# Strassen's algorithm for the gate and up products of two 512-feature blocks in each SwiGLU of a two-layer encoder trunk, with the feed-forward loops written out

## The reference, cut to what matters

```python
def _swiglu(h, w_gate, w_up, w_down):
    return (jax.nn.silu(h @ w_gate) * (h @ w_up)) @ w_down
...
        x = x + 0.5 * _swiglu(_rms_norm(x, ffn1_norm[l]), ffn1_w_gate[l], ffn1_w_up[l], ffn1_w_down[l])
```

## Time and profile before

| | us |
|---|---|
| median of 3 runs | 1047.45 (1047.15 to 1047.8) |
| span of the profiled execution, first to last instruction | 1045.7 |
| TensorE busy | 1040.6 |
| VectorE busy | 687.1 |
| ScalarE busy | 593.7 |
| DMA, mean | 200 GB/s, 208.81 MB |

### The profile page before, as it was taken

How to read it: one execution, slowest core, us unless ns; L and a number is a source line. 1 busy time by engine, 2 the same in 40 slices (tenths; PEclk the granted TensorE clock), 3 DMA queues, 4 the chain that set the end, 5 groups by cost and what they waited for, 6 DMA issues and landing times.

```text
span 1045.7 us, 13767 instructions
## 1 busy us (share of the span) xinstructions
PE 1040.6 (100%) x5001; PEld 872.2 (83%) x5001; DVE 687.1 (66%) x911; ACT 593.7 (57%) x792; POOL 248.9 (24%) x258
## 2 busy tenths in 40 slices
PE   9999999999999999999999999999999999999998
PEld 6888888998888888888888888889988888888887
DVE  6755655698976766555576555656999677656551
ACT  6754544576874665445466454536778557645440
POOL 2960000148850000000048300002588300000000
PEclk9999999999999999999999999999999999999999
DMA  8977666455644696675569667565366366976641
GB/s 280 310 237 234 186 211 200 143 200 172 210 163 125 206 313 188 206 232 196 153 191 282 216 206 228 184 199 172 122 212 224 118 191 222 261 221 186 207 139 41
DMA packets 191555, 208.81 MB, mean 200 GB/s; under 512 B 64112, under 2 KB 162704, under 8 KB 191504
## 3 DMA queue, kind: packets, MB, share of 16 engines
q1 hardware_dynamic: 190288, 206.03, 63.6%
q10 hardware_dynamic: 1216, 2.11, 0.7%
HBM read 192.90 MB, written 1.05 MB: 185 GB/s over the span
## 4 chain that ended last, share of the span: by engine, by line
PE 98%; ACT 1%; DVE 1%; issue 0%; POOL 0%; ACTq 0%
PE bank L663 31%; PE bank L665 31%; PE bank L664 31%; PE bank L744 1%; PE bank L905 1%; PE bank L914 1%; PE bank L935 1%; PE bank L670 1%; PE bank L702 0%; PE bank L913 0%; PE bank L937 0%; DVE htok L1563 0%; DVE x L1611 0%; ACT htok L1132 0%; PE bank L923 0%; PE bank L963 0%
## 5 line engine op out<-in xcount | busy, mean ns | idle before, releaser
L1517 DVE TENSOR_TENSOR wlo<-raw,whi 128x2048 fp32r<-128x2048 f32 (+2 forms) x152 | 347.4, 2290 | 82.6 <-ACT whi L1123 81.5
L663 PE MATMUL bank<-whi,hThi 128*128 128x512 f32 (+1 forms) x976 | 378.4, 388 | 0.0
L665 PE MATMUL bank<-whi,hTlo 128*128 128x512 f32 (+1 forms) x976 | 373.7, 383 | 0.0
L664 PE MATMUL bank<-wlo,hThi 128*128 128x512 f32 (+1 forms) x976 | 373.6, 383 | 0.0
L1123 ACT ACTIVATE whi<-raw 128x2048 fp32r<-128x2048 f32 (+2 forms) x176 | 335.3, 1910 | 16.8 <-DMA raw<-in_ffn_w_up 7.3
L665 PEld LDWEIGHTS bank<-whi,hTlo 128*128 128x128 f32 x976 | 183.3, 188 | 35.7
L663 PEld LDWEIGHTS bank<-whi,hThi 128*128 128x128 f32 x976 | 183.4, 188 | 35.1 <-issue 0.3
L664 PEld LDWEIGHTS bank<-wlo,hThi 128*128 128x128 f32 x976 | 183.4, 188 | 34.8
L1216 ACT ACTIVATE gates<-bank,small 128x256 f32<-128x256 f32 x88 | 41.8, 475 | 263.5 <-PE bank L665 262.8
L663 PE MATMUL bank<-whi,gThi 128*128 128x512 f32 (+1 forms) x416 | 162.2, 390 | 0.0
L664 PE MATMUL bank<-wlo,gThi 128*128 128x512 f32 (+1 forms) x416 | 161.1, 387 | 0.0
(11 more groups left out here) (177 smaller groups left out, 823.6 us busy)
## 6 DMA issues: line engine op xcount, KB each, us to landing
raw<-in_ffn_w_down SPq DMA_DIRECT2D x88, 512.0 KB, 4.2
raw<-in_ffn_w_gate SPq DMA_DIRECT2D x84, 512.0 KB, 4.3
raw<-in_ffn_w_up SPq DMA_DIRECT2D x84, 512.0 KB, 5.4
raw<-in_w_in SPq DMA_DIRECT2D x48, 512.0 KB, 4.8
raw<-in_w_out SPq DMA_DIRECT2D x16, 512.0 KB, 4.4
raw<-in_w_in SPq DMA_DIRECT2D x8, 544.0 KB, 4.5
raw<-in_w_mla_out SPq DMA_DIRECT2D x8, 512.0 KB, 3.9
raw<-in_w_conv_out SPq DMA_DIRECT2D x8, 512.0 KB, 4.7
```

Of the source, the lines that this page charges most:

```text
L663: nc.tensor.matmul(out, lh, rh, start=start, stop=False, skip_group_check=skip)
L664: nc.tensor.matmul(out, lh, rl, start=False, stop=False, skip_group_check=skip)
L665: return nc.tensor.matmul(out, ll, rh, start=False, stop=stop, skip_group_check=skip)
L1517: nc.vector.tensor_tensor(wlo[:, slot(u0, RING), 0:n], raw[:, slot(u0, RAW), 0:n], whi[:, slot(u0, RING), 0:n].bitcast(F32), ALU.subtract) ...
```

## The change

In each feed-forward, chunks 3 and 4 together, and 6 and 7 together, become one block of 512 features. With A the input (two row tiles by two channel halves) and B the weights (gate and up, 512 columns each, by two channel halves), four quarters each, the block's [gate up] is A times B by Strassen's algorithm in Winograd's form: 7 products of a 128 x 512 quarter with a 512 x 512 quarter instead of 8, each 4 k-steps x 3 matmuls. Three of them take a weight quarter as it is (B11, B22, B21), four take sums of quarters (T1 to T4).

- **Weights.** The upper quarters of gate and up go to two buffers of their own (chain[0], chain[1], over htok and ktok) and not to the raw slots. VectorE forms T1, T3, T2 and T4 in place (`add_T1` and so on, 128x2048 each); ScalarE rounds and VectorE takes the remainder of each of the 7 as a unit.
- **Inputs.** Once in each feed-forward VectorE adds hThi and hTlo (`whole_rows`, 128x2048), makes four mixed quarters (`mixed_rows`, 4 of 128x512), ScalarE rounds them (`mixed_round`, 128x2048) and VectorE takes the remainder (`mixed_rest`, 128x2048).
- **Outputs.** Within a block ScalarE copies four banks out (`keep`, 128x512), VectorE does four sums of 128x512 (`up_first`, `gate_first`, `up_second`, `gate_second`), two silus and two gated products of 128x512 replace four of each of 128x256. Both row tiles of both chunks are complete only after T4.
- **Orders.** All loops are written out, with a new order of calls on each engine. gain, bias, vtok and cu share one region with the mixed input quarters; cu's margin is cleared once a layer. Units, raw slots and counters are renumbered for this.

Within the lists below, `gate_split`, `down_split` and `lower` are the same ScalarE or VectorE steps as `split` before, for a unit of gate and up, of w_down, and for B22 and B21; `first_of` and `sum_of` are ScalarE's rounding of chain buffers, `of_chain` VectorE's remainder of them. The hunks stand in the order SP, TensorE, ScalarE, VectorE, after the constants.

```diff
--- before.py
+++ after.py
+BLK = (3, 6)
+CW = 2 * FC
+PRODUCTS = ("B11", "T1", "D0", "T2", "B22", "B21", "T3", "T4", "D1")
...
+        chain = (htok[:, 0:2048], heads[:, 0:2048])
...
+        mixed = flat[:, 512:2560].rearrange("p (k n) -> p k n", k=KD)
+        kept = [flat[:, 512 + i * CW:512 + (i + 1) * CW] for i in range(4)]
...
+                b = per_block(l, f, c) - 1
+                if b % len(BLK) == 0:
+                    if i == 0:
+                        sp.wait_ge(sq_ready, per_norm(l, 2 * f, 1))
+                    elif l or f:
+                        sp.wait_ge(block_joined[1], nth_norm(l, 2 * f, 0) + 1)
+                else:
+                    last = unit_block(f, BLK[b % len(BLK) - 1], "T3" if i else "T4")
+                    sp.wait_ge(wlo_ready, l * U_LAYER + last + 1)
+                dst = chain[i].rearrange("p (k n) -> p k n", k=4)
+                src = quarter_of((wg, wu)[i][f], l, c, 0)
+                for k in (0, 2):
+                    sp.dma_start(dst[:, k:k + 2, :], src[:, k:k + 2, :]).then_inc(chain_landed[i], 16)
...
+                gate_up(l, f, 2, 0)
+                gate_up(l, f, 2, 1)
+                down(l, f, 0)
+                chain_load(l, f, 3, 0)
+                down(l, f, 1)
+                chain_load(l, f, 3, 1)
+                lower_load(l, f, 3, "B22")
+                turn(0)
+                lower_load(l, f, 3, "B21")
+                turn(1)
+                turn(2)
+                down(l, f, 2)
+                gate_up(l, f, 5, 0)
+                gate_up(l, f, 5, 1)
+                chain_load(l, f, 6, 1)
+                chain_load(l, f, 6, 0)
+                down(l, f, 3)
+                down(l, f, 4)
+                lower_load(l, f, 6, "B22")
+                turn(3)
...
+                def block_product(c, name, b, lhs, start=True, stop=True):
+                    u = unit_block(f, c, name)
+                    unit_waits(pe, l, u)
+                    for k in range(4):
+                        ins = products(bank[:, b, :], lhs(k), wt(u, 2048, 4, k, slice(0, CW)),
+                                       start=start and k == 0, stop=stop and k == 3, skip=True)
+                    ins.then_inc(unit_free, 1)
+                def mixed_T(h, t):
+                    def of(k):
+                        cols = slice(t * P, (t + 1) * P)
+                        return sThi[:, 4 * h + k, cols], sTlo[:, 4 * h + k, cols]
+                    return of
+                def strassen(c):
+                    done = per_block(l, f, c)
+                    again = c != BLK[0]
+                    def plain_T(h, t):
+                        return lambda k: hT(4 * h + k, t)
+                    if again:
+                        pe.wait_ge(kept_ready, (done - 1) * 4)
+                    else:
+                        pe.wait_ge(gu_ready, per_gu(l, f, 2, 0))
+                    block_product(c, "B11", 4, plain_T(0, 0))
+                    if again:
+                        pe.wait_ge(c12_ready, done - 1)
+                    else:
+                        pe.wait_ge(gu_ready, per_gu(l, f, 2, 1))
+                        pe.wait_ge(mixed_ready, l * 2 + f + 1)
+                    block_product(c, "T1", 5, mixed_T(1, 1))
+                    down(c - 2, 0)
+                    down(c - 2, 1)
+                    pe.wait_ge(kept_ready, (done - 1) * 4 + 1)
+                    block_product(c, "T2", 4, mixed_T(0, 0), start=False)
+                    pe.wait_ge(kept_ready, (done - 1) * 4 + 2)
+                    block_product(c, "B22", 5, mixed_T(1, 0), start=False)
+                    pe.wait_ge(gu_ready, per_gu(l, f, 5 if again else 1, 0))
+                    block_product(c, "B21", 6, plain_T(1, 0))
+                    pe.wait_ge(kept_ready, (done - 1) * 4 + 3)
+                    block_product(c, "T3", 4, mixed_T(0, 1), start=False)
+                    pe.wait_ge(gu_ready, per_gu(l, f, 5 if again else 1, 1))
+                    block_product(c, "T4", 7, plain_T(1, 1))
+                    down(c - 1, 0)
+                    down(c - 1, 1)
...
                 first()
-                pair(2, 2)
-                pair(3, 3)
-                with pe.Fori(0, (NCH - 5) // 2) as i:
-                    pair(i * 2 + 4, 4)
-                    pair(i * 2 + 5, 5)
+                pair(2)
+                strassen(3)
+                pair(5)
+                strassen(6)
+                pair(8)
+                pair(9)
                 last()
...
+                def mixed_round():
+                    act.wait_ge(mix_step, (l * 2 + f + 1) * 5)
+                    nc.scalar.activation(sThi[:, :, :], mixed, ACT.Copy).then_inc(mixed_hi, 1)
...
+                def block_first(c):
+                    sum_of(c, "T2")
+                    lower(c, "B22")
+                    lower(c, "B21")
+                    keep(c, 0, "B11")
+                    sum_of(c, "T3")
+                    keep(c, 1, "T1")
+                    sum_of(c, "T4")
+                    round_joined(c - 1)
+                    down_split(c - 1)
+                    keep(c, 2, "T2")
+                    gate_split(c + 2, 0)
+                    gate_split(c + 2, 1)
...
+                def block_second(c):
+                    block_silu(c, 0)
+                    keep(c, 3, "T3")
                     split_planes(c, 0)
-                    silu(c, 1)
-                    split(l, u + 2, i)
+                    down_split(c)
+                    block_silu(c, 1)
                     split_planes(c, 1)
                 first()
...
-                    pair(i * 2 + 2, 2, i * 2)
-                    pair(i * 2 + 3, 3, i * 2)
+                down_split(0)
+                silu(1, 0)
+                first_of(3, "B11")
+                split_planes(1, 0)
+                round_joined(0)
+                mixed_round()
+                silu(1, 1)
+                split_planes(1, 1)
+                sum_of(3, "T1")
+                silu(2, 0)
+                down_split(1)
+                split_planes(2, 0)
+                silu(2, 1)
+                round_joined(1)
+                split_planes(2, 1)
+                block_first(3)
+                block_second(3)
+                first_of(6, "B11")
+                split_planes(4, 0)
+                split_planes(4, 1)
+                round_joined(3)
...
+                def mixed_rows():
+                    n = (l * 2 + f) * 5
+                    dve.wait_ge(mix_step, n + 1)
+                    mix(quarter(1, 1), quarter(0, 1), quarter(1, 1), ALU.subtract)
+                    mix(quarter(0, 1), quarter(0, 0), quarter(0, 1), ALU.subtract)
+                    dve.wait_ge(mix_step, n + 2)
+                    mix(quarter(0, 0), quarter(1, 1), quarter(0, 0), ALU.subtract)
+                    dve.wait_ge(mix_step, n + 4)
+                    mix(quarter(1, 0), quarter(1, 0), quarter(0, 0), ALU.add)
+                def mixed_rest():
+                    dve.wait_ge(mixed_hi, l * 2 + f + 1)
+                    rest(sTlo[:, :, :], mixed, sThi[:, :, :]).then_inc(mixed_ready, 1)
...
+                def block_second(c):
+                    up_first(c)
+                    down_split(c - 1)
+                    gate_first(c)
+                    up_second(c)
+                    gate_split(c + 2, 0)
+                    block_mul(c, 0)
+                    gate_second(c)
+                    gate_split(c + 2, 1)
+                    block_mul(c, 1)
+                    down_split(c)
...
-                with dve.Fori(0, (NCH - 3) // 2) as i:
-                    pair(i * 2 + 2, 2, i * 2)
-                    pair(i * 2 + 3, 3, i * 2)
+                    gate_split(1, 1)
+                    gate_split(2, 0)
+                    gate_split(2, 1)
+                    mul(0, 1)
+                whole_rows()
+                mul(1, 0)
+                mixed_rows()
+                down_split(0)
+                join(0)
+                mul(1, 1)
+                rest_joined(0)
+                of_chain(3, "B11")
+                add_T1(3)
+                mul(2, 0)
+                mixed_rest()
+                add_T3(3)
+                mul(2, 1)
+                of_chain(3, "T1")
+                join(1)
+                add_T2(3)
+                rest_joined(1)
+                down_split(1)
+                of_chain(3, "T2")
+                add_T4(3)
+                join(2)
+                lower(3, "B22")
+                lower(3, "B21")
+                rest_joined(2)
+                of_chain(3, "T3")
+                of_chain(3, "T4")
+                block_second(3)
+                of_chain(6, "B11")
+                add_T1(6)
+                join(3)
+                add_T3(6)
+                rest_joined(3)
+                mul(5, 0)
+                of_chain(6, "T1")
+                join(4)
+                add_T2(6)
+                mul(5, 1)
+                rest_joined(4)
+                down_split(4)
```

(94 more changed lines are left out.)

402 lines of the change are left out of this document (266 added, 136 removed).

## The result

The changed kernel takes **1095.65 us** (median of 4 runs, 1090.01 to 1096.83) for 1047.3 before on the same chip: a ratio of 1.0453, 95% interval 1.0437 to 1.0468. The prediction was 1089, with 1062 to 1112 around it. The profiled execution has a span of 1095.0 us for 1045.7. Two executions further down, one of 4725.78 us in experiment 6 and one of 3741.64 us in experiment 8, fell in a slow state and are left out of the ratios.

The account below looks back on a forecast made before the run. TensorE, busy 1040.6 of 1045.7 us, was taken to bound the kernel before, with VectorE slower inside blocks. From 1047.45, 21.8 us saved against 63.8 of waits (3 x 15.3 + 17.9), net +42.0, gave 1089.5; range 1062 to 1112.

Parts of the forecast that it names:

- signs of being wrong: TensorE's waits below 22 us, a long one elsewhere (down(3) over 4, or block 6), or granted clock under 1 outside the start.
- What TensorE saves: Two blocks in four feed-forwards: 96 matmuls less, 21.8 us, giving 1025.7 without any wait.
- The crossed waits: First block: VectorE stands still 3.0 us for silu(1,1) and 2.4 for silu(2,0), by the order of calls; 5.4 together.
- The queued transpose: At join(0): the transpose, behind five loads, lands at 376, between 368.5 and 378; 2.5 us with hand-overs.
- rival 1: At join(0): transposes not delayed by loads, 2.5 us less in three feed-forwards, 3.7 in the first: 1078; chance 10%.
- The first block: Feed-forward 2: T1 starts 9.1 us late, down(1) 12.4 late at 401.9; 3.4 of the 12.4 is work.
- After T4: From T4's remainder to down(3): VectorE needs 23.1 us, so down(3) starts 2.9 us late (between 0 and 4).
- Block 6 worked the same way gives no wait: Second block: gate_up(5) costs VectorE two remainders, down(6) is wanted 0.5 to 1 us after it is ready; no wait.
- Rival 2: Gaps between 378.6 and 401.9: the clock falls, matmuls slow, some 5 us per feed-forward: 1109; chance 18%.
- Rival 3: At T1 and down(1): VectorE keeps ahead, the saving stands; 1045 with pure work alone, 1026 without waits; chance 8%.
- Costed at nothing: Whole kernel: longer rows, chain loads, written-out loops, moved buffers, renumbered slots and cu's memset add no time.

Follow-up runs that it names:

- experiment 6: Experiment 5's kernel with VectorE's remainders of down(1) and chunk 1 ahead of sum T2, sum T4 and join of chunk 2 later: 1052.87 us.
- experiment 8: The kernel before with its three chunk loops written out and nothing else changed: 1047.27 us, ratio 0.9999.
- experiment 1: The changed kernel with ScalarE's silu(1,1) ahead of its planes, rounding and mixed_round, and silu(2,0) ahead of its rounding of T1: 1074.6 us.
- experiment 2: The changed kernel with SP issuing the transpose of chunk 0 ahead of the loads of chain[1] and B22: 1082.45 us.
- experiment 7: The changed kernel with VectorE's remainder of chunk 6 ahead of the second remainder of unit gate 9: 1088.84 us.
- experiment 3: The changed kernel with TensorE multiplying zeros, 16 products between B11 and T1 and 9 before down(3), in each feed-forward: 1092.13 us.
- experiment 5: The changed kernel with the reorderings of experiment 1, experiment 2 and experiment 7, plus VectorE's join and remainder of chunk 3 one weight sum earlier: 1046.83 us.
- experiment 11: The kernel of experiment 10 with ScalarE, in both blocks, copying T3 before the first silu and taking the second silu before rounding down(c): 1041.84 us.
- 9: Experiment 6's kernel with ScalarE's copies of products B11 and T1 ahead of its rounding of sum T2 and units B22 and B21: 1055.92 us.
- experiment 12: Experiment 5's kernel with experiment 11's ScalarE order, without zeros, and the first block's sum T3 on GpSimd: 1052.5 us.
- 10: Experiment 5's kernel with TensorE running 8 products of zeros behind T1 of the first block: 1046.37 us.

## Why the prediction was right, and where it was off

The direction and the mechanism held, and the time lies 6 us above the forecast, inside the range. That it is so near is in part luck: waits that were counted too long and long steps that were not counted at all offset each other. Two of the prediction's own signs of being wrong came: waits in block 6 and a granted clock under 1 outside the start.

- **What TensorE saves**: 4905 matmuls, as worked out. Nothing speaks against the 21.8 us.
- **The crossed waits**: 3.0 and 2.4 were forecast in feed-forward 2, 2.92 and 2.34 are there, and experiment 1 gave back 21.0 us, against 4 x 5.4 = 21.6. They are a fact of order alone. What stayed in that run, 2.4 to 3.5 us before T1, the forecast would have given to VectorE's work and the transpose.
- **The queued transpose**: it landed at 388.1, 375.1 on before's clock, for the 376 taken. The trace rules out rival 1, which had the transposes undelayed (9.5 us from issue to join, for 3.0 to 4.3 in the earlier trace rows), and experiment 2 shows that the loads ahead of it are what delays it.
- **The first block**: in feed-forward 2 down(1) starts 10.3 us late instead of 12.4 (412.83, 399.8 on before's clock, for 389.5). Two terms were mis-sized. The transpose was 0.9 early; and back to back, VectorE starts a remainder every 2.20 us (392.75 to 394.96), where each had been given 2.29. That is 0.09 for each of some ten operations. The earlier trace rows show it already, 362.09 to 364.30, and the sum for the first feed-forward used 2.21 once. Before down(1) 3 us of waiting were forecast; there are 1.2 to 1.6, and in front of them T1's long steps, 1.2 to 1.6 us, fill part of the same time.
- **After T4**: 2.9 late was forecast, 2.9 to 3.3 is in the trace of feed-forwards 2 to 4, and 2.5 in the first. From its first product to down(3) a feed-forward lost 15.0, 13.4, 14.5 and 14.8 us, 57.7 in all, for the 63.8 forecast.
- **The step that failed**: "Block 6 worked the same way gives no wait", with down(6) wanted "0.5 to 1 us after it is ready". TensorE waits 1.1 to 1.7 us before down(6) in each feed-forward. That step counted VectorE's work, but not what its remainder of gate 9 waits for (experiment 7): the same crossing of orders that the first block's walk had found, in a place that was not walked through. It cost 6.8 us by the run.
- **Rival 2, the clock**: some 15 us of longer steps in the trace, for the 20 of the rival, though only 3.5 us came back when the gaps were filled (experiment 3). The forecast left it at nothing, which is the second term that failed; it was between the two. The 0.43 us steps from 407.77 on, at a granted clock of 0.51, stand behind a wait of 4.07. The Trainium skill (TensorE: Matmul & The Clock Gate, Part 1) has the clock halve after idling, and the trace agrees. How much of it is hidden behind VectorE only the runs tell.
- **Rival 3, VectorE keeps ahead**: it gave 1045 for a first block without crossed waits. With the orders mended the runs come to the same number, 1046.8 (experiment 5), but not by the rival's sum: it had 19.2 us of waits, 5.6 of them before down(3), and edit 5 has 14 us of waits, none before down(3), and 7 of long steps. 1041.8 came with two more pauses of VectorE removed and the gap filled (experiment 11), so 1045 was no floor. What is left in the first block is shown by the stretch up to down(1), where VectorE is 96% busy. That its work bounds the rest too, and so that the full saving (1026) is out of reach, is not shown.
- **Costed at nothing**: the loops, rightly (experiment 8). The moved buffers and the longer rows of the loads were not tried on their own.

In sum: the waits were forecast at 63.8 and are 54, though 5.6 of these, before down(6), were forecast at nothing; lengthened steps were forecast at 0 and are 15.

## What to carry to other kernels

When a change gives more work to an engine that feeds the bound one, write down the order of both helping queues side by side and look for pairs that each has in the other's opposite order: here such crossings, one transpose queued behind loads and one sum in the wrong place cost the whole 48 us, on engines 60 and 77% busy, and mending the order alone took it back (experiment 5). Walk through every stretch that the change touches, not only the worst. When a gap only moves as orders are changed, don't take that for a bound by work: look how busy the engine is in that stretch and what its own pauses wait for (after experiments 6 and 9 had moved the gap about, two such pauses still gave 4.5 us in experiment 11). Where it is busy throughout, only less work helps, and the engine that takes the work over must not hold up the one that is to be relieved (experiment 12).

## What the runs showed of the hardware

- A transpose issued behind loads in flight kept SP's queue for 5.03 us (4.3 to 5.5 in the four feed-forwards of the changed kernel), against 1.23 with two loads fewer ahead of it (experiment 2).
- In the changed kernel, behind the waits of 2.4 to 4.1 us (as the brackets give them) before T1, down(3) and, in the first feed-forward, down(0), six to nine matmuls stepped at 0.43 us instead of 0.2267, 1.2 to 1.6 us each time. Behind its waits of 1.0 to 2.3 us none did, but in experiments 1 and 7 eight or nine did behind a wait of 1.9, so the length of the wait alone does not tell. Filling the gap with products of zeros kept the step short (experiments 3, 10).
- A GpSimd sum of 128x2048 (4.63 us) held up a VectorE remainder of the same shape for 4.27 us (experiment 12).
